# A transformer kernel's opening: the order of the first loads, tiles, warming and squares

## The reference

```python
km, vm = jnp.split(mem @ w_mem_kv, 2, axis=-1)     # for layer a and layer b; keys and values, 256 columns each
h = rms_norm(x, pre_norm[0])                        # x * rsqrt(mean(x*x) + eps) * gain
h @ w_in_even                                       # the first mixer's projections: e_av (512 columns) comes first
```

## Time and profile before

| what | us |
|---|---|
| median of the 3 runs shown (lowest, highest) | 941.76 (941.01, 944.14) |
| the profiled execution's own time | 941.11 |
| its span, from the first to the last instruction | 939.3 |
| PE busy in the span | 901.2 |
| DVE busy | 650.4 |
| ACT busy | 489.0 |
| POOL busy | 41.5 |

### The profile page before, as it was taken

How to read it: one execution, slowest core, us unless ns; L and a number is a source line. 1 busy time by engine, 2 the same in 40 slices (tenths; PEclk the granted TensorE clock), 3 DMA queues, 4 the chain that set the end, 5 groups by cost and what they waited for, 6 DMA issues and landing times.

```text
span 939.3 us, 14616 instructions
## 1 busy us (share of the span) xinstructions
PE 901.2 (96%) x5650; PEld 774.3 (82%) x5650; DVE 650.4 (69%) x1182; ACT 489.0 (52%) x890; POOL 41.5 (4%) x73
## 2 busy tenths in 40 slices
PE   8999999899998899999999999998999999999997
PEld 8888987688986788767888888887897788888885
DVE  5659585756666646857697678676664778768676
ACT  5454274456666456644455454544654455455441
POOL 2005000100001100000000000000000000000000
PEclk9999999989999999999999999999999999999999
DMA  8845434364362752111656655547242356555561
GB/s 310 297 143 166 153 113 141 129 224 158 113 198 77 285 188 91 68 46 68 202 179 202 189 196 179 186 169 244 94 156 95 131 202 222 184 190 184 186 202 45
DMA packets 45504, 155.06 MB, mean 165 GB/s; under 512 B 5404, under 2 KB 8060, under 8 KB 45436
## 3 DMA queue, kind: packets, MB, share of 16 engines
q1 hardware_dynamic: 40688, 141.78, 44.6%
q10 hardware_dynamic: 4748, 12.36, 4.1%
HBM read 152.78 MB, written 1.34 MB: 164 GB/s over the span
## 4 chain that ended last, share of the span: by engine, by line
PE 82%; DVE 9%; ACT 5%; issue 1%; POOL 1%; DMA 1%; DVEq 0%; ACTq 0%; SPq 0%
PE ps L2035 16%; PE ps L2050 13%; PE ps L791 7%; PE ps L2034 7%; PE ps L684 5%; PE ps L685 5%; PE ps L686 5%; PE ps L701 4%; PE ps L703 3%; PE ps L702 3%; PE ps L871 3%; PE ps L880 2%; PE ps L923 2%; DVE wlo L652 2%; PE ps L803 1%
## 5 line engine op out<-in xcount | busy, mean ns | idle before, releaser
L652 DVE TENSOR_TENSOR wlo<-raw,whi 128x1024 fp32r<-128x1024 f32 (+1 forms) x263 | 313.5, 1215 | 30.6 <-ACT whi L646 30.1
L646 ACT ACTIVATE whi<-raw 128x1024 fp32r<-128x1024 f32 (+1 forms) x263 | 271.3, 1046 | 90.4 <-DMA raw<-in_ws 36.7
L2035 PE MATMUL ps<-t,whi 128*128 128x512 f32 x640 | 221.6, 396 | 0.0
L2034 PE MATMUL ps<-t,wlo 128*128 128x256 f32 x560 | 156.2, 279 | 0.0
L684 PE MATMUL ps<-t,whi 128*128 128x256 f32 (+1 forms) x480 | 140.4, 293 | 0.3 <-ACT arena L1665 0.3
L685 PE MATMUL ps<-t,whi 128*128 128x256 f32 (+1 forms) x480 | 136.5, 284 | 0.0
L686 PE MATMUL ps<-t,wlo 128*128 128x256 f32 (+1 forms) x480 | 136.4, 284 | 0.0
L2035 PEld LDWEIGHTS ps<-t,whi 128*128 128x128 f32 x640 | 115.9, 188 | 22.5
L2034 PEld LDWEIGHTS ps<-t,wlo 128*128 128x128 f32 x560 | 105.6, 189 | 3.6
L2050 PE MATMUL ps<-whi,r 128*128 128x512 f32 x352 | 98.0, 390 | 0.0
L684 PEld LDWEIGHTS ps<-t,whi 128*128 128x128 f32 (+1 forms) x480 | 92.3, 192 | 6.4 <-issue 4.3
(11 more groups left out here) (268 smaller groups left out, 1280.7 us busy)
## 6 DMA issues: line engine op xcount, KB each, us to landing
raw<-in_ws SPq DMA_DIRECT2D x256, 512.0 KB, 4.1
vecs<-in_vecs ACTq DMA_DIRECT2D x12, 512.0 KB, 6.1
arena<-in_ws ACTq DMA_DIRECT2D x5, 512.0 KB, 6.6
raw<-in_ws SPq DMA_DIRECT2D x4, 384.0 KB, 3.5
tb<-brow ACTq DMA_DIRECT2D x8, 192.0 KB, 5.4
rows<-in_mem SPq DMA_DIRECT2D x2, 512.0 KB, 4.0
x<-in_x SPq DMA_DIRECT2D x1, 1024.0 KB, 10.1
rows<-in_ws ACTq DMA_DIRECT2D x2, 512.0 KB, 7.6
```

What stands on the lines that cost most here:

```text
L646: a.i.activation(whi[:, j % NSPLIT, 0:n], raw[:, j % NRAW, 0:n], ACT.Copy).then_inc(*a.sig("hi", u))
L652: d.i.tensor_tensor(wlo[:, j % NSPLIT, 0:n], raw[:, j % NRAW, 0:n], whi[:, j % NSPLIT, 0:n].bitcast(F), ALU.subtract).then_inc(*d.sig("lo" ...
L2034: p.i.matmul(ps[:, b, 0:T], wl[:, k, :], thi[:, k, :], start=False, stop=False)
L2035: mm = p.i.matmul(ps[:, b, :], wh[:, k, :], t2[:, k, :], start=k == 0, stop=k == 7)
```

## The change

The memory's first values, `mv0`, become the first two units of the stream, ahead of the keys, and `mv1` stays behind them. The SP queue issues them between and behind the two halves of the memory; x's load moves behind the third unit. `START` is written anew: it now begins with the memory's own transposes, then both row blocks of `mv0` unit by unit. Squares of x, half by half, stand at the two "rms" entries on ACT. The load of vectors 1 and 2 is an entry "vecs" of its own, behind the last key tile. ACT runs one small copy as its first instruction, which brings its table load there. The warming is 8 matmuls at first and 6 behind each half of the transposes. `dve_rms` can split a unit between the product with the gain and the wait for the root. `mv0` and `mv1` are now held each from their own first unit.

```diff
+    chunk("mv0", "a_w_mem_kv_2", span(256, 256))
     for z, nm in enumerate(("a", "b")):
         tiles(f"mk{z}", f"{nm}_w_mem_kv_2", span(0, 256))
-    for z, nm in enumerate(("a", "b")):
-        chunk(f"mv{z}", f"{nm}_w_mem_kv_2", span(256, 256))
+    chunk("mv1", "b_w_mem_kv_2", span(256, 256))
...
-    held.update({u: U["mv0"][0] for u in U["mv0"] + U["mv1"]})
+    held.update({u: U[name][0] for name in ("mv0", "mv1") for u in U[name]})
...
-    in_turn(*each("mk0"), *each("mk1"), *both("mv0"), *both("mv1"))
+    in_turn(*both("mv0"), *each("mk0"), *each("mk1"), *both("mv1"))
...
-    def dve_rms(d, key, q, *given):
+    def dve_rms(d, key, q, *given, upto=0):
         dve_gained(d, key, q, lambda n: x[:, q, half[n]], *given)
+        dve_split(d, upto)
         d.wait_ge("root", key, q)
...
-    START = [("tile", "mk0", 0), ("rms", 0), ("tile", "mk0", 1), ("tile", "mk1", 0), ("rms", 1), ("tile", "mk1", 1)]
-    START += by_rows("mv0", 0) + by_rows("mv1", 0) + [("T", 1, 0)] + by_rows("mv0", 1) + [("rt", 0, 0)] + by_rows("mv1", 1)
+    START = [("T", 0, 0), ("T", 0, 1)] + [("chunk", "mv0", k, q) for k in range(2) for q in range(2)]
+    START += [("tile", "mk0", 0), ("rms", 0), ("tile", "mk0", 1), ("tile", "mk1", 0), ("rms", 1), ("tile", "mk1", 1), ("vecs",)]
+    START += by_rows("mv1", 0) + [("T", 1, 0), ("rt", 0, 0)] + by_rows("mv1", 1)
...
-        for q in range(2):
-            s.i.dma_start(rows[:, q, :], inp["mem"][q * P:q * P + P, :]).then_inc(*s.sig(f"c_mem{q}", "all", by=16))
-        sp_loads(s, range(0, 2))
+        s.i.dma_start(rows[:, 0, :], inp["mem"][0:P, :]).then_inc(*s.sig("c_mem0", "all", by=16))
+        sp_loads(s, range(0, 1))
+        s.i.dma_start(rows[:, 1, :], inp["mem"][P:2 * P, :]).then_inc(*s.sig("c_mem1", "all", by=16))
+        sp_loads(s, range(1, 3))
         s.i.dma_start(x[:, :, :], inp["x"].rearrange("(b p) d -> p b d", p=P)).then_inc(*s.sig("c_x", "all", by=16))
-        sp_loads(s, range(2, 7))
+        sp_loads(s, range(3, 7))
...
         p.wait_ge("c_ident", "all")
-        for q in range(2):
-            if q == 0:
-                pe_warm(p, 8, 7)
-            p.wait_ge(f"c_mem{q}", "all")
-            pe_rows_t(p, 0, q)
-        pe_warm(p, 8, 3)
-        p.wait_ge("tlo", 0, 3)
+        pe_warm(p, 4, 7)
...
             elif what == "T":
+                if a[0] == 0:
+                    p.wait_ge(f"c_mem{a[1]}", "all")
                 pe_rows_t(p, *a)
+                if a[0] == 0:
+                    pe_warm(p, 3, 3)
...
-        a.wait_ge("c_mem1", "all")
-        act_vec(a, 0)
-        for q in range(2):
-            act_rows_t(a, 0, q)
-        act_split(a, AHEAD - 1)
-        a.wait_ge("c_x", "all")
-        a.wait_ge("tp", 0, 3)
-        for q in range(2):
-            act_squares(a, "pre0", q, lambda n: x[:, q, half[n]])
+        a.wait_ge("nhalf", 0)
+        a.i.activation(st("bag0", 8)[:, 0:1], nhalf[:, 0:1], ACT.Copy).then_inc(*a.sig("table", 0))
         for what, *k in START:
             if what in ("tile", "chunk"):
                 u, q = unit_of(what, k)
-                act_split(a, ahead(u, q))
+                act_split(a, u + 1 if u < 4 else ahead(u, q))
...
             elif what == "T":
                 act_rows_t(a, *k)
-            elif what == "rms" and k[0] == 1:
+                if k == [0, 0]:
+                    act_split(a, 0)
+                elif k == [0, 1]:
+                    act_vec(a, 0)
+            elif what == "rms":
+                a.wait_ge("c_x", "all")
+                a.wait_ge("tp", 0, 3)
+                act_squares(a, "pre0", k[0], lambda n: x[:, k[0], half[n]])
+            elif what == "vecs":
                 a.wait_ge("hrow", "pre0", 1, 1)
                 for i in range(1, 3):
                     act_vec(a, i)
...
     def dve_start(d):
-        for q in range(2):
-            dve_rows_t(d, 0, q)
+        d.wait_ge("c_ident", "all")
         d.i.tensor_reduce(quarters[:, :], ident[:, :].rearrange("p (g n) -> p n g", g=4), AX, ALU.add).then_inc(*d.sig("quarters", 0))
...
-                dve_split(d, ahead(u, q))
+                dve_split(d, u + 2 if u < 4 else ahead(u, q))
...
-                dve_rms(d, "pre0", a[0])
+                dve_rms(d, "pre0", a[0], upto=5 + a[0])
             elif what == "T":
                 dve_rows_t(d, *a)
+                if a == [0, 0]:
+                    dve_split(d, 1)
```

## The result

The changed kernel is slower: 944.99 us median (943.27 to 946.32) against 941.71 for the kernel before (941.01 to 944.14), seven runs each; ratio 1.0027, 95% interval [1.0014, 1.0040]. Measured a second time, beside other kernels, it was 1.0035 [1.0019, 1.0052]. The forecast was 942.0, with a range to 943.9. So next to no difference was predicted, and 3.3 us by the medians, 2.5 by the first ratio, were lost. The profiled execution took 945.14 us, its span is 943.3, 4.0 more than before.

A forecast was written before the change was run, and what follows sets the result against it. PE following itself was taken as the bound (82% of the span). Terms -2.75 +1.15 +1.85 = +0.25 us on the profiled 941.11 gave 941.4, or 942.0 for the measured median; range 939.3 to 943.9.

The forecast's parts named there:

- PE's start: Opening: first projection matmul at 10.15 instead of 12.91 us, priced at -2.75 us.
- The wait for lo 4: Near 22 us PE waits for DVE's remainder of load 4, delayed by x's first squares on ACT: +1.15 us.
- The second root: Before `e_av`, GpSimd's root for x's second half holds DVE's work until 31.8, so PE stands idle: +1.85 us.
- Each of these I cost at nothing: Other moved pieces (small tables, `decay` to `conv`, load 12, vectors 1 and 2, buffers freed earlier): priced at zero.
- the tail 42.35 to 44.59 stays 2.2: From x's second transposes to `e_av`'s second row block: unchanged at 2.2 us.
- the queue is emptier; 40 at the latest, needed at 42.6: Load 12, issued at 33.9 instead of 33.04 us, would still land in time, at no cost.
- rival (b): New PE stalls near 21.8 and 35.3 bring a granted clock of 0.50: 943.7 to 945.3 us; chance 0.10.
- the one near 35.3: PE's forecast stall before `e_av`'s first block, 1.85 us, from 35.3 to 37.15.
- (a): The gain stays: `e_av` starts when PE is free, at 35.3: 940.2 us, or 939.0 at best; chance 0.28.
- (c): PE's start isn't earlier: memory's second half lands after 7.7, or first block waits for lo 0; 943; chance 0.07.

The follow-up runs named there:

- the kernel with the order repaired: Changed kernel with x's second transposes copied ahead of hi 12 and hi 13 (ACT's and DVE's splits of units 12 and 13 held back), no load moved: 941.37 us, ratio 0.9990.
- the second run with the squares earlier: Changed kernel with x's first squares on ACT ahead of the first key tile's evacuation, measured a second time: 944.45 us, ratio 1.0021 to the kernel before.
- The tables and vectors experiments: Changed kernel with seven constant tables issued behind loads 12 and 13 (941.32 us, 0.9991); separately, with vectors 1 and 2 behind x's second transposed copies (941.82 us, 0.9999).

## Why the prediction was wrong

*PE's start*, -2.75: measured -2.09. The links were right; the slow clock lasted some tenths longer in this execution, and the memory's second half let the transposes begin at 8.63 and not at 7.95. In the kernel with the order repaired the start was at 10.25, in the second profile of the changed kernel at 11.72: single executions differ by more than the term was off.

*The wait for lo 4*, +1.15: measured 1.12, at the place and for the reason given. ACT evacuated at 19.74, squared, and began hi 4 at 21.25. From start to start of PE's matmuls it cost some 1.35, since the ends that the 1.12 is read from are modelled; with that the first links add up to the -0.73 at `e_av`.

*The second root*, +1.85: not there. The root took 0.96 us and not 1.9. The 1.9 was read from rows where GpSimd's first instruction took 1.24; now it took 0.3:

```profile
21.44 0.32 POOL L1116 TENSOR_SCALAR stat<-stat 128x1 f32<-128x1 f32 x1 [18.27 <-ACT sm L1100]
...
29.68 0.30 POOL L1116 TENSOR_SCALAR stat<-stat 128x1 f32<-128x1 f32 x1 [7.27 <-ACT sm L1100]
30.07 0.56 POOL L1119 TENSOR_TENSOR stat<-stat,nhalf 128x1 f32<-128x1 f32 x1
```

In both places DVE stood idle meanwhile, at first until hi 4 (2.71 us, to 22.32), the second time until the root itself (1.71 us):

```profile
22.32 1.23 DVE L652 TENSOR_TENSOR wlo<-raw,whi 128x1024 fp32r<-128x1024 f32 x1 [2.71 <-ACT whi L646]
...
30.66 0.88 DVE L1136 TENSOR_SCALAR rows<-rows,stat 128x512 f32<-128x512 f32 x2 [1.71 <-POOL stat L1119]
```

Load 8 took 3.38 and not 4.3, and PE itself was free only at 36.1, so the wait vanished. The term was mis-sized, and what was left of it was covered, by luck, by a later PE: in the second run with the squares earlier PE was free at 35.25 and did wait 0.95.

*"Each of these I cost at nothing"* is the step that failed, and with it "the tail 42.35 to 44.59 stays 2.2": from the transposes to the second block it was 5.40. The prediction said of load 12 "the queue is emptier; 40 at the latest, needed at 42.6", and of the vectors only when they are first used. Load 13, which ACT's written order puts ahead of x's second transposes as well, has no price in it at all. Load 12 landed at 42.86 and load 13 at 44.10. The queue was the fuller: load 8 and 9 had moved 1.7 and 2.5 us to later, the vectors 6.6, and the DMA engines stood part idle from 20 to 32. I had followed each transfer by its own latency and never added the bytes. The price of this: +3.16 in place of 0. The tables and vectors experiments each remove it, and so does the order. The cover that the prediction named, that `e_av`'s first block runs on loads already split, was there; what it doesn't cover is ACT, which waits for the loads in its turn.

*The clock*, rival (b): its price, 1.5 to 3.25 (its sum then took 1.7 to 3.3), was right, and 1.52 was paid. Its place was not: the clock fell after the 4.37 us at the transposes. After the stall that came at 23.70 it stayed at 1.00, and the one near 35.3 did not come.

*Rivals (a) and (c)*: (a) came true as far as 41.62, since `e_av` did start when PE was free, and was lost one step further on. (c) came true in small: the memory's second half landed at 8.59 and not at 7.7, and PE waited 0.23 for it. Its sign, a first matmul after 11, stands in the second profile of the changed kernel. Yet its second block starts at 47.03, as in the first: with load 13 landing at 44.11 the start no longer counts.

The check that was missing is a sum of bytes against time. When load 13 landed, 13.4 MB were through in the kernel before (at 41.66) and 13.7 MB in the changed one (at 44.10). At the 393 GB/s of full engines that is 34 and 35 us, so the time that the DMA engines left unused ahead of it grew from 7.6 to 9.2 us. It was left unused early, and from 32 us on full engines could not make it up. Whether that sum, made with the prediction's own times, would have given 44 for load 13 and not 40 is open.

## What to carry to other kernels

Where the DMA engines are full for a stretch, as here from 32 us to load 13's landing, reckon a reordering in bytes by a time, not in latencies of single transfers: a transfer that nobody waits for still holds an awaited one that is asked for shortly behind it. Asked for earlier or behind it, the same bytes cost nothing that could be measured here. An engine that works in order should do what its consumer waits for before it waits for anything prefetched; here that order cost nothing until a load was late, and then all of it. Filler that covers a wait is not always waste: taken away alone it gained nothing, and the clock fell in its profile.

## What the runs showed of the hardware

GpSimd's small `TENSOR_SCALAR` on 128x1 took 1.24 us at 17.89 in the kernel before, while DVE multiplied two SBUF tensors, as this row of its timeline before shows, and 0.32 and 0.30 in the changed kernel with DVE idle.

```profile
17.75 1.29 DVE L1127 TENSOR_TENSOR rows<-x,vecs 128x512 f32<-128x512 f32 x2
```

The second root of the kernel before shows the same of GpSimd's next instruction: 1.44 us beside DVE's subtraction of two SBUF tensors (from 20.63 on), and 0.57 and 0.56 in the changed kernel with DVE idle.

```profile
20.83 1.44 POOL L1119 TENSOR_TENSOR stat<-stat,nhalf 128x1 f32<-128x1 f32 x1
```

The Trainium skill (GPSIMD Engine Reference, 1. Specifications) says that GpSimd shares its SBUF interfaces with VectorE and contends with instructions of two SBUF inputs; these rows agree, though no run was made for this alone.

The same 2.15 us stall of PE behind `e_av`, between 58 and 66 us, was followed by a granted clock of 0.50 in seven of the fourteen profiles and of 1.00 in the other seven, and the changed kernel is on both sides. So which of the two comes after a stall of about 2 us differs from execution to execution, and a difference of 1.7 us between single executions can be that alone.
